# A decoder trunk's last rounds: eight scalings moved behind the first arithmetic on the last products, one table load, row products begun with the running sum

## The reference, cut to what matters

```python
def rms_norm(x, w):
    y = x * lax.rsqrt(jnp.mean(x * x, axis=-1, keepdims=True) + EPS)
    return y * w

# x: (1, 1024, 2048), p: (1, 1, 1024, 256), one layer
u = rms_norm(x, norm_mix_w)
# ... projection, two groups of gated linear attention, y ...
h = x + y @ w_out
e = rms_norm(p @ ple_proj, ple_norm_w)
gate = sigmoid(rms_norm(h, ple_gate_norm_w) @ ple_gate_w + ple_gate_b)
h = h + gate * e
return rms_norm(h, final_norm_w)
```

## Time and profile before

| what | value |
|---|---|
| median of 3 executions | 2166.76 us (2165.82 to 2166.89) |
| the profiled execution | 2165.31 us, span of its instructions 2163.4 us |
| TensorE busy | 2138.2 us (99%), 10234 matmuls |
| VectorE busy | 1500.5 us (69%) |
| ScalarE busy | 997.9 us (46%) |
| GpSimd busy | 165.4 us (8%) |
| mean granted TensorE clock | 0.993 of 2.4 GHz |
| chain that ended last | PE 94%, DVE 3%, issue 1%, DMA 1% |
| HBM | 339.88 MB read, 139.72 MB written |

### The profile page before, as it was taken

One profiled execution on the slowest core, in us unless ns is written; L12 is line 12 of the kernel. 1 busy time (PEld: TensorE's weight loads), 2 busy tenths in 40 slices (PEclk: granted clock), 3 DMA queues, 4 the chain that ended last, 5 costly groups with the idle time before them and its releaser, 6 DMA issues.

```text
span 2163.4 us, 30191 instructions
## 1 busy us (share of the span) xinstructions
PE 2138.2 (99%) x10234; PEld 1790.7 (83%) x10234; DVE 1500.5 (69%) x2973; ACT 997.9 (46%) x1746; POOL 165.4 (8%) x244
## 2 busy tenths in 40 slices
PE   9999999999999999999999999999999999999995
PEld 7888888888888888888888888888888888888885
DVE  7577777776666677777676655566667777786887
ACT  7355454453343354444444434334455455432553
POOL 1001100010000000010101011000010000000110
PEclk9999999999999999999999999999999999999997
DMA  9525666664554455354536566344497685898876
GB/s 329 186 97 166 165 168 170 172 173 152 138 166 123 137 150 147 102 171 120 166 106 185 167 181 175 98 140 134 132 310 271 210 268 196 266 262 284 237 198 205
DMA packets 130266, 390.65 MB, mean 181 GB/s; under 512 B 15040, under 2 KB 20544, under 8 KB 128832
## 3 DMA queue, kind: packets, MB, share of 16 engines
q1 hardware_dynamic: 108736, 283.56, 39.2%
q0 software_dynamic: 21440, 105.92, 20.6%
HBM read 339.88 MB, written 139.72 MB: 222 GB/s over the span
## 4 chain that ended last, share of the span: by engine, by line
PE 94%; DVE 3%; issue 1%; DMA 1%; ACT 0%; SPq 0%; ACTq 0%; DVEq 0%; POOLq 0%
PE acc L952 24%; PE acc L954 24%; PE acc L953 24%; PE lv L1045 3%; PE tr L954 2%; PE ms L954 2%; PE tr L953 2%; PE ms L953 2%; PE tr L952 2%; PE ms L952 2%; PE so L1054 1%; PE so L1034 1%; PE so L1057 1%; PE ms L1023 1%; DVE w_lo L1792 1%
## 5 line engine op out<-in xcount | busy, mean ns | idle before, releaser
L952 PE MATMUL acc<-act_hi,w_lo 128*128 128x512 f32 x2384 | 956.4, 401 | 1.6 <-DVE feat L2226 0.7
L954 PE MATMUL acc<-act_hi,w_hi 128*128 128x512 f32 x2384 | 928.0, 389 | 0.0
L953 PE MATMUL acc<-act_lo,w_hi 128*128 128x512 f32 x2384 | 927.5, 389 | 0.0
L1268 ACT CAST w_hi<-w_raw 128x1024 fp32r<-128x1024 f32 x339 | 343.4, 1047 | 457.3 <-PE acc L954 338.5
L954 PEld LDWEIGHTS acc<-act_hi,w_hi 128*128 128x128 f32 x2384 | 447.5, 188 | 94.5
L952 PEld LDWEIGHTS acc<-act_hi,w_lo 128*128 128x128 f32 x2384 | 448.6, 188 | 89.7 <-issue 4.5
L953 PEld LDWEIGHTS acc<-act_lo,w_hi 128*128 128x128 f32 x2384 | 448.8, 188 | 84.3 <-issue 1.0
L1792 DVE TENSOR_TENSOR w_lo<-w_raw,w_hi 128x1024 fp32r<-128x1024 f32 x339 | 402.8, 1221 | 121.5 <-ACT w_hi L1268 116.3
L1344 ACT ACTIVATE work<-work 128x512 f32<-128x512 f32 x120 | 75.6, 630 | 146.5 <-DVE work L1848 145.9
L1862 DVE COPY_PREDICATED work<-mask_sb,lv 128x256 f32<-128x256 uint8 x168 | 88.8, 528 | 7.4
L1282 ACT ACTIVATE work<-work 128x512 f32<-128x512 f32 x64 | 40.5, 632 | 95.8 <-DVE work L1828 95.8
(11 more groups left out here) (371 smaller groups left out, 2485.9 us busy)
## 6 DMA issues: line engine op xcount, KB each, us to landing
w_raw<-in_slabs SPq DMA_DIRECT2D x276, 512.0 KB, 4.4
w_sums<-in_slabs POOLq DMA_DIRECT2D x96, 512.0 KB, 5.9
w_raw<-w_sums SPq DMA_DIRECT2D x64, 512.0 KB, 5.1
w_sums<-w_sums POOLq DMA_DIRECT2D x32, 512.0 KB, 4.0
work<-e_scratch SPq DMA_DIRECT2D x56, 256.0 KB, 5.0
t_sums<-y_scratch POOLq DMA_DIRECT2D x24, 512.0 KB, 7.2
feat<-in_x_feat SPq DMA_DIRECT2D x8, 1024.0 KB, 11.7
e_scratch<-work SPq DMA_DIRECT2D x32, 256.0 KB, 6.2
```

The costliest lines, as they stand in the source:

```text
L952: nc.tensor.matmul(ps, lhs_lo, rhs_hi, start=start, stop=False)
L953: nc.tensor.matmul(ps, lhs_hi, rhs_lo, start=False, stop=False)
L954: return nc.tensor.matmul(ps, lhs_hi, rhs_hi, start=False, stop=stop)
L1268: nc.scalar.copy(w_hi[par][:, j, :], w_raw[j][:, :]).then_inc(w_hi_ready, 1)
```

## The change

Six edits, all in the last rounds:

- `SCALES_AT` keeps eight tiles (two, three, three in rounds 23, 24, 25); `LATE_SCALES`, tiles 8 to 15, are scaled in the tail: two after the first products of part 1, six after the gates of part 1. Before, round 25 scaled four, round 26 four, and round 27 three. SP stores them behind everything else of half 0, as they come.
- In every round that has both a tile (n, 0) and a tile (n-1, 0), `g_add(before[0])` stands before `g_sum_up` of tile (n, 0), where it stood at the round's end.
- In the tail VectorE takes the last products (`z_product`) first, and the last two `g_embed` and two of the `g_add` come between and behind.
- ScalarE does all four sigmoids before the table load for logarithm and exponential. One load is left of three.
- `row_products` is ordered by addend, running sum first, each with its own wait, into four PSUM columns in two banks instead of two and two; the variance is one instruction a column. It is called after the product loop and no longer as a hook in it.
- On PE `row_products(1)` stands before `by_token(0)`.

```diff
-        z_rows = [so_ps[0][:, 0:2], acc[1][:, PART:PART + 2]]
+        z_rows = [[so_ps[u][:, part:part + 1] for u in range(2)] for part in range(2)]
-        SCALES_AT = {23: range(0, 2), 24: range(2, 5), 25: range(5, 9), 26: range(9, 13), 27: range(13, KT)}
+        SCALES_AT = {23: range(0, 2), 24: range(2, 5), 25: range(5, 8)}
+        LATE_SCALES = range(8, KT)
@@ SP
-            for u in SCALES_AT[GATE_SLABS - 1]:
+            for u in LATE_SCALES:
                 store_out(0, u)
@@ PE
+                def blocks(sq_tile, start=False, stop=False):
+                    for u in range(2):
+                        toks = slice((2 * part + u) * C, (2 * part + u + 1) * C)
+                        last = nc.tensor.matmul(z_rows[part][u], sq_tile[:, toks], ones[:, 0:1], start=start, stop=stop)
+                    return last
+
                 pe.wait_ge(g2_ready, 2 * KT - 2)
+                blocks(g_sum[1], start=True)
+                pe.wait_ge(z_sq, 2 * part + 1)
+                blocks(z_1[0])
                 pe.wait_ge(z_sq, 2 * part + 2)
-                for u in range(2):
...
-                last.then_inc(rows_ready, 1)
+                blocks(z_1[1], stop=True).then_inc(rows_ready, 1)
...
-                          21: {10: lambda: row_sums(ROWS_F[0], g2_ready, KT, g_sum[0])},
-                          27: {15: lambda: row_products(0)}}
+                          21: {10: lambda: row_sums(ROWS_F[0], g2_ready, KT, g_sum[0])}}
...
+            row_products(0)
             factors(0)
+            row_products(1)
             by_token(0)
-            row_products(1)
             factors(1)
             by_token(1)
@@ ACT
-            for part in range(2):
...
+            z_sigmoid(0, 0)
+            z_sigmoid(0, 1)
+            z_square(0, 0)
+            z_square(0, 1)
+            z_sigmoid(1, 0)
+            z_sigmoid(1, 1)
+            act.preload_act_table_set("natural_log_exp_and_others")
+            z_rsqrt(0)
+            z_square(1, 0)
+            z_square(1, 1)
+            z_rsqrt(1)
@@ DVE
                         g_embed(G_NO[n, 0])
+                        if before:
+                            g_add(before[0])
                         g_sum_up(G_NO[n, 0])
...
-                    if before:
+                    if before and (n, 0) not in G_NO:
                         g_add(before[0])
                     st.fresh()
-            for j in range(2):
-                g_embed(LAST - 1 + j)
-            g_add(LAST - 3)
-            g_add(LAST - 2)
-            for u in SCALES_AT[GATE_SLABS - 1]:
-                f_scale(u)
...
             z_product(0, 0)
             z_product(0, 1)
+            g_embed(LAST - 1)
+            g_add(LAST - 3)
+            g_add(LAST - 2)
+            st.wait()
             z_gate(0, 0)
+            g_embed(LAST)
+            st.wait()
             z_gate(0, 1)
+            z_product(1, 0)
+            z_product(1, 1)
+            for u in LATE_SCALES[0:2]:
+                f_scale(u)
             z_variance(0)
             z_factor(0)
-            z_product(1, 0)
-            z_product(1, 1)
-            z_scale(0, 0, 4)
             z_gate(1, 0)
             z_gate(1, 1)
-            z_scale(0, 4, KT - N_TOK)
+            for u in LATE_SCALES[2:]:
+                f_scale(u)
+            z_scale(0, 0, 4)
             z_variance(1)
             z_factor(1)
+            z_scale(0, 4, KT - N_TOK)
             z_scale(1, 0, KT - N_TOK)
```

## The result

The changed kernel took 2171.16 us as median of 11 executions (2166.78 to 2180.2), the kernel before beside it on the same chip 2166.08 (2163.89 to 2169.64): ratio 1.0024, 95% interval 1.0015 to 1.0033. In a second comparison it took 2169.27 against 2166.53, 1.0014 (1.0005 to 1.0023). So it is 3 to 5 us slower where I had forecast 0.7, and the first median lies outside my range (2163.3 to 2170.0). The profiled execution took 2171.47 us, its span is 2169.3.

What follows compares the result with a forecast made beforehand. VectorE paces TensorE and the stores set the end: a 2.5 us lag, then a shorter tail, left VectorE 1.8 ahead, lost in the store queue; 0.7 added to 2166.76 gave 2167.5 us, range 2163.3 to 2170.0.

Steps and rivals of the forecast that it cites:

- Part 1: Add moved ahead of the gated sum: it waits for ScalarE's square, so VectorE loses 0.48 us a round.
- rounds 5 to 7, where VectorE has slack that rounds without embedding restore: The moved add also sits in these early rounds; its loss there was taken as absorbed, costing nothing later.
- lag at slab 27: +2.5: Rounds 17 to 25: 4.32 us lost, less 1.19 of waits for TensorE and 0.66 for round 25's dropped scaling.
- Parts 2 to 5: Tail: later scalings, one table load, reordered row products, stores setting the end; VectorE's 1.8 us gain lost in the store queue.
- the table load at 1.28 with no drain: ScalarE's one remaining load in the tail takes 1.28 us and holds the first logarithm back 0.3.
- row products off the path: Tail: rows come at about 2137.6, before VectorE reaches the variance at 2139.2, so their order and clock don't count.
- Free add: Rival: the moved add costs nothing, square early or lag taken up; span 2160.4, median 2163.8 us; 14%.
- Stores don't bind: Rival: the end follows the last scaling by 4.93 us as before, so 1.8 faster, 2165.0; 14%.
- load of 2.66: Rival: the table load includes a drain, VectorE idles 1.38 us longer after the first variance; 2168.9; 7%.
- add waits for a DMA: Rival: the square waits for the residual's DMA to land, each round losing the excess; 2169.8 to 2172.0 us; 12%.
- The clock: Rival: TensorE's clock falls in the wait ahead of slab 25; half-speed products cost up to 10.9 us, half gives 2173; 3%.
- The wait of 2 ahead of slab 25: Sign that the forecast is right: TensorE waits about 2 us there, as VectorE's lag shows.

Runs made afterwards that it cites:

- the heavier version: Changed kernel with the add back at the round's end, plus two more VectorE products in each of rounds 5, 6 and 7: 2170.85 us, ratio 1.0027.
- the square first: Changed kernel with ScalarE making the square of tile (n-1, 0) ahead of the sigmoid of tile (n, 0): 2160.3 us, ratio 0.9975.
- the kernel in which it is free: Changed kernel with the add put back at the end of the round, all else kept: 2163.85 and 2163.78 us, ratio 0.9994 both times.

## Why the prediction failed where it did

**Part 1, the mechanism: right.** The add waits for a square that stands behind the sigmoid; the sum comes 1.24 later (forecast 1.20). The nine rounds take 106.2 with the move (four profiles) and 101.7 without it (mean of seven, all with three scalings in round 25): 4.5, so 0.50 a round against 0.48. In three of the seven VectorE still waits for TensorE, but the four that don't have nearly the same mean, 101.5.

**Part 1, "rounds 5 to 7, where VectorE has slack that rounds without embedding restore": this step failed.** VectorE loses 1.72 in them (2.56 behind before at the end of round 4, 4.28 at the end of round 7), and no slack of later rounds can be relied on to restore it. Shown is that for the larger loss: 4.57 there were 7.1 at round 17 in the heavier version. For the 1.72 it is only likely. Profiles with these rounds moved have round 17 at 204.9 on average (six), those without at 203.3 (six, 202.30 to 204.33; the square first and the heavier version left aside), but the groups overlap: two of the moved ones stand at 203.0 and 203.1. The medians agree with that: where rounds 17 to 26 have the move, leaving it out of rounds 5 to 7 gives 2168.43 in place of 2169.27 to 2172.01; where they don't, it changes nothing that can be seen.

**Part 1, the sum "lag at slab 27: +2.5": mis-sized, and by the way it was built.** I took the starting point of round 17 from one profile and let the waits of the earlier trace rows absorb 1.19. From that starting point the sum is nearly right: 106.2 against 103.36 are +2.85. But its 202.30 is the earliest of the six profiles that leave rounds 5 to 7 and ScalarE's order alone, by 0.6 to 2.0; the kernel before itself was profiled once. In that kernel a start later by 1 us makes no difference, because VectorE waits for TensorE as late as round 21, 1.19 in all. In the changed kernel it counts in full. So the forecast lacked 1.0 (203.3 instead of 202.30), 1.6 for rounds 5 to 7 (204.9 instead of 203.3), 0.35 in the rounds and 0.14 ahead of the tail: 3.1 on 2167.5 is 2170.6, between the two medians, 2171.16 and 2169.27. These are means of few profiles; that the parts fit so well is partly luck. The second profile shows how much of it is chance: it has round 17 at 203.0, and its execution took 2167.37, 1.4 above the 2166.0 that I had forecast for a profiled one. The spread is no proof either: executions of the changed kernel lie 13 us apart in the first comparison and 7.5 in the second, those of before 6 in both.

TensorE's lag of 2.57 ahead of the gate stage is no part of the change's cost. The same program began that stage at 1811.93 in one profile and 1809.78 in the other.

**Parts 2 to 5: right**, each within 0.3: the distances in the tail, the 12.84 from low weights to first arithmetic (12.7), the table load at 1.28 with no drain (0.02 to the logarithm), row products off the path, full DMA engines at the end, and 7.14 from the last scaling to the end (forecast 7.4).

**The rivals.** *Free add* was given 2163.8; the kernel in which it is free measured 2163.85 and 2163.78. *Stores don't bind*, *load of 2.66* and *add waits for a DMA* fell: the idle time is 1.38 in each round and its releaser the square, which starts as the sigmoid ends (2117.08, after 2116.45 + 0.72). *The clock*: it did fall, in slab 21 and not ahead of slab 25, and cost nothing: profiles without it have the same 106.2 us for rounds 17 to 26. The wait of 2 ahead of slab 25 that I forecast stands in the second profile (2.05 between two starts); in the first it had been spent in slab 21. I gave slower by over 0.2% only 8%, and the first run is slower by 0.24%, the second by 0.14%.

## What to carry to other kernels

Before an operation is moved into a wait, look up what it needs itself and where that stands in its own engine's order: here the two must move together, and then 3 to 5 us lost become 6 gained (2.1 to 2.3 of them by the rest of the change). A term that "is absorbed" needs its slack named and counted over several executions, for a change that uses up slack turns every late arrival into time. Where the end is set by the stores, shorten what fills the queue last, not the arithmetic ahead of it.

## What the runs showed of the hardware

- A VectorE instruction with two operands in SBUF stood for 10.79 us while GpSimd ran eight products with two operands back to back (10.20). The Trainium skill ("SBUF — State Buffer", SBUF: two separate sides) has the shared port pair held for one whole instruction by whoever starts first. The trace agrees that one of the two stands, but not on how long or on the order: VectorE's instruction is recorded 0.03 us ahead of the first of GpSimd's (2118.06 and 2118.09) and still ended last, and between the eight, 1.28 each on average, it got no turn.
- TensorE's granted clock fell to 1.2 GHz (0.57 of 2.4 on average from 2062 to 2066) after the engine had stood for 2.55 us in the middle of a busy stream, and was at 1.00 again in the window from 2066. The forecast had seen no return in the trace before.
- A table load of ScalarE took 1.28 us in all eight cases of the trace before and all six after, and where the next instruction was ready it started 0.01 behind it; no drain was seen.
